# A decoder layer in fp32: attention summed by parts, and eight gate tiles moved ahead of it

## The reference

```python
z = jnp.einsum('bhqd,bhkd->bhqk', qb, kb).astype(jnp.float32) * scale
mask = kpos < qpos
log_beta = jax.nn.log_sigmoid(z)
log_1m_beta = jnp.where(mask, jax.nn.log_sigmoid(-z), 0.0)
log_a = log_beta + lax.cumsum(log_1m_beta, axis=3, reverse=True) - log_1m_beta
a = jnp.where(mask, jnp.exp(log_a), 0.0)
outs.append(jnp.einsum('bhqk,bhkd->bhqd', a.astype(vb.dtype), vb))
...
g = jax.nn.sigmoid(gate_logits.astype(jnp.float32)).astype(u.dtype)
g_pool, g_sb = jnp.split(g, 2, axis=-1)
return (g_pool * y_pool + g_sb * y_sb) @ w_out
```

## Time and profile before

| | us |
|---|---|
| median of 3 runs (lowest, highest) | 1923.49 (1922.86, 1924.46) |
| the profiled execution, its own time | 1924.59 |
| its span in the profile | 1922.6 |
| TensorE busy | 1908.7 |
| VectorE busy | 1399.9 |
| ScalarE busy | 789.2 |
| GpSimd busy | 152.4 |

### The profile page before, as it was taken

The page is one execution under the profiler, slowest core; times in us unless marked ns, Lnnn a source line. Parts: engine busy times, 40 slices in busy tenths (PEclk is TensorE's granted clock), DMA queues, the critical chain, the costliest instruction groups (busy, mean ns, idle before and its releaser), DMA issues.

```text
span 1922.6 us, 25206 instructions
## 1 busy us (share of the span) xinstructions
PE 1908.7 (99%) x9034; PEld 1596.7 (83%) x9034; DVE 1399.9 (73%) x1723; ACT 789.2 (41%) x1175; POOL 152.4 (8%) x221
## 2 busy tenths in 40 slices
PE   9999999999999999999999999999999999999998
PEld 9888888888888888888888888898888888888886
DVE  6977867774566776786878878889777777755655
ACT  7423232323434543345566652474323232334344
POOL 1000000000000300002443420010000000000002
PEclk9999999999999999999999999999999999999999
DMA  5456654558676534248546347643545444677665
GB/s 165 147 198 228 225 175 149 190 194 310 206 241 197 185 110 149 74 134 231 147 120 182 101 148 254 198 137 114 183 140 198 148 168 153 221 262 242 204 195 199
DMA packets 246724, 347.19 MB, mean 181 GB/s; under 512 B 16368, under 2 KB 150256, under 8 KB 243056
## 3 DMA queue, kind: packets, MB, share of 16 engines
q1 hardware_dynamic: 246640, 346.10, 55.0%
HBM read 232.79 MB, written 112.98 MB: 180 GB/s over the span
## 4 chain that ended last, share of the span: by engine, by line
PE 95%; DVE 3%; issue 1%; DMA 1%; ACT 0%; POOL 0%; SPq 0%; DVEq 0%; POOLq 0%; ACTq 0%
PE bank L1248 39%; PE bank L1357 10%; PE bank L1304 9%; PE bank L1305 9%; PE bank L1306 9%; PE bank L1498 4%; PE bank L1200 3%; PE bank L1406 2%; PE bank L1434 2%; PE bank L1464 2%; PE bank L1570 2%; PE bank L1175 1%; PE bank L1589 1%; PE bank L1588 1%; PE bank L1555 1%; PE bank L1553 1%
## 5 line engine op out<-in xcount | busy, mean ns | idle before, releaser
L2232 DVE TENSOR_TENSOR dn_lo<-dn_lo_raw,dn_hi 128x1024 fp32r<-128x1024 f32 x149 | 181.9, 1223 | 150.5 <-ACT dn_hi L1773 149.9
L1248 PE MATMUL bank<-lo_t,wa_hi 128*128 128x512 f32 x656 | 252.8, 389 | 0.0
L1248 PE MATMUL bank<-hi_t,wa_lo 128*128 128x512 f32 x656 | 252.8, 389 | 0.0
L1248 PE MATMUL bank<-hi_t,wa_hi 128*128 128x512 f32 x656 | 252.8, 389 | 0.0
L1773 ACT ACTIVATE dn_hi<-dn_lo_raw 128x1024 fp32r<-128x1024 f32 x149 | 157.9, 1061 | 218.3 <-DMA dn_lo_raw<-act_dram 218.3
L1304 PE MATMUL bank<-dn_hi 128*128 128x512 f32 x596 | 232.6, 390 | 0.0
L1306 PE MATMUL bank<-dn_lo,dn_hi 128*128 128x512 f32 x596 | 231.9, 389 | 0.0
L1305 PE MATMUL bank<-dn_hi,dn_lo 128*128 128x512 f32 x596 | 231.9, 389 | 0.0
L1248 PE MATMUL bank<-hi_b,wa_hi 128*128 128x512 f32 x492 | 190.7, 390 | 1.8 <-DVE up L2366 1.8
L1248 PE MATMUL bank<-lo_b,wa_hi 128*128 128x512 f32 x492 | 190.4, 389 | 0.0
L1248 PE MATMUL bank<-hi_b,wa_lo 128*128 128x512 f32 x492 | 190.4, 389 | 0.0
(11 more groups left out here) (276 smaller groups left out, 3722.7 us busy)
## 6 DMA issues: line engine op xcount, KB each, us to landing
wa_lo_raw<-in_ffn_w_gate_up_dram SPq DMA_DIRECT2D x87, 512.0 KB, 5.0
dn_lo_raw<-act_dram SPq DMA_DIRECT2D x149, 256.0 KB, 4.4
act_dram<-g SPq DMA_DIRECT2D x44, 512.0 KB, 4.3
wd_t<-in_ffn_w_down_dram SPq DMA_DIRECT2D x44, 512.0 KB, 6.6
act_dram<-s_of SPq DMA_DIRECT2D x88, 256.0 KB, 6.5
wd_dram<-wd_t SPq DMA_DIRECT2D x22, 1024.0 KB, 6.0
dn_lo_raw<-wd_dram SPq DMA_DIRECT2D x85, 256.0 KB, 3.3
dn_lo_raw<-in_ffn_w_down_dram SPq DMA_DIRECT2D x64, 256.0 KB, 3.0
```

Source lines behind the costliest of these rows:

```text
L1248: last = nc.tensor.matmul(acc, lhs, rhs, start=n == 0 and i != 2 and i < 5, stop=n == 11, skip_group_check=True)
L2232: return nc.vector.tensor_tensor(dst, raw, hi.bitcast(f32), ALU.subtract)
```

## The change

Three things are changed.

1. Summation by parts. In place of the weight of each key, its running sum from the right is made: one scan over `keep` and `a` (r = keep * r + a), written over `a`. The products then take differences of neighbouring values, v[s] - v[s-1], in place of the values. So `weigh_keys` loses its product, GpSimd masks `a` alone, the values are stored whole in DRAM behind a row of zeros (`v_dram`), and are loaded with and without a shift by one row (`load_v`), subtracted (`differences`) and split (`differences_hi`, `differences_lo`), for each of the four pairs of heads.
2. `EARLY = 8`: the eight tiles of the attention gate are made by four more units of seven products in `MIX_UNITS`, ahead of attention. In attention stand the eight tiles of the pooling gate, in four units of two tiles (`GATE_UNITS`), 16 banks. `SHARE` is changed, and still sums to 788 with the rest.
3. In the second feed-forward part, VectorE's second pair of units is written out as `second_pair`, with another order in its first unit.

```diff
-EARLY = 0
+EARLY = 8
 GATE_UNITS = tuple(((0, j), (0, j + 1)) for j in range(0, EARLY, 2)) + tuple(((0, j), (1, j)) for j in range(EARLY, KT))
...
+V_DIFF, V_HIGH, V_LOW = ({NT + 3 + d: 1, 3 * NT + 3 + d: 2, 5 * NT + 3 + d: 3} for d in (0, 1, 5))
...
-SHARE = {7: 8, 6: 16, 1: 16, 0: 11, 5: 4, 4: 12, 3: 13, 2: 12}
+SHARE = {7: 8, 6: 14, 1: 14, 0: 11, 5: 10, 4: 11, 3: 12, 2: 12}
...
-        v_dram = nc.dram_tensor("v_dram", (2, P, 2 * SEQ), f32, kind="Internal").ap()
+
+        v_dram = nc.dram_tensor("v_dram", (1 + SEQ, BR, P), f32, kind="Internal").ap()
...
+            def load_v(k):
+
+                if k >= 2:
+                    sp_.wait_ge(pv_ok, NT * (k - 1))
+                elif k == 0:
+                    for i in range(4):
+                        sp_.wait_ge(v_sp[i], 32)
+                    for i in range(3):
+                        sp_.wait_ge(ring_sp[i], 32 * ring_uses(i))
+                    sp_.wait_ge(ylo, 4)
+                    sp_.wait_ge(v_in[0], 16)
+                for a, row in ((0, 1), (1, 0)) if k >= 2 else ((1, 0),):
+                    for e in range(2):
+                        sp_.dma_start(v_raw[:, k % 2, :, e, a, :],
+                                      v_dram[row:row + SEQ, PAIR_ORDER[k], e * HD:(e + 1) * HD].rearrange("(t p) c -> p t c", p=P)
+                                      ).then_inc(v_in[k % 2], 16)
...
-                for pair in range(2):
-                    if s == NT * (2 + 2 * pair) + 4:
-                        load_v(pair)
+                for k in (1, 2, 3):
+                    if s == (2 * NT * (k - 1) + 4 if k > 1 else 2):
...
-                if x_["pair"] < 2 and pn % NT == 0:
-                    pe.wait_ge(v_in[slot], 16)
+                if pn % NT == 0:
+                    pe.wait_ge(v_split, 3 * (pn // NT) + 3)
...
-                nc.scalar.activation(v_w[:, :, t, :, 0, :], acc[:, 1], ACT.Copy)
-                if t > 4:
-                    act.wait_ge(v_sp[b], 16)
-                nc.scalar.activation(value_place(t)[:, :, :, 0, :], acc[:, 0], ACT.Copy).then_inc(ev_hi, 1)
+                nc.scalar.activation(v_raw[:, :, t, :, 0, :], acc[:, 1], ACT.Copy).then_inc(ev_hi, 1)
...
+            def differences_hi(k):
+
+                act.wait_ge(v_split, 3 * k + 1)
+                nc.scalar.activation(v_w[:, k % 2, :, :, 0, :], v_raw[:, k % 2, :, :, 1, :], ACT.Copy).then_inc(v_split, 1)
...
+                if s in V_HIGH:
+                    differences_hi(V_HIGH[s])
...
+                    second_pair(even, odd, units)
+                    with dve.Fori(2, KF - 2) as i:
                         pair_units(i, wd_use(1, i - 1))
...
+            def second_pair(even, odd, units):
+
+                c11(1, 2, 0)
+                weight_sums(1, 3, odd, units + 2)
+                c22_first(1, 2, 0)
+                weights_lo(1, 3, odd)
+                c22_second(1, 2, 0)
                 sums_of_pair(1, 0, lambda: dve.wait_ge(summed, 7 * strassen(1, 1) + 7))
+                sums_lo(1, 3, odd)
+                unit_end(1, 2, 1, 0, wd_use(1, 0))
+                up_unit(1, 3, 1, 1, more=(even, units + 3))
 
...
-                acc = bank[:, (t + 4) % 8, :].rearrange("p (m s e c) -> p m s e c", m=2, s=2, e=2)
-                nc.vector.tensor_tensor(v_w[:, :, t, :, 1, :], acc[:, 1], v_w[:, :, t, :, 0, :].bitcast(f32), ALU.subtract)
-                nc.vector.tensor_tensor(value_place(t)[:, :, :, 1, :], acc[:, 0], value_place(t)[:, :, :, 0, :].bitcast(f32),
-                                        ALU.subtract).then_inc(acc_free[t % 4], 1)
+                if t > 4:
+                    dve.wait_ge(v_sp[t % 4], 16)
+                nc.vector.tensor_copy(value_place(t), bank[:, (t + 4) % 8, :]).then_inc(acc_free[t % 4], 1)
...
+            def differences(k):
+
+                slot = k % 2
+                dve.wait_ge(v_in[slot], (32, 96)[k // 2] + (0 if slot else 16))
+                now, before = (v_raw[:, slot, :, :, a, :] for a in range(2))
+                nc.vector.tensor_tensor(before, now, before, ALU.subtract).then_inc(v_split, 1)
+
+            def differences_lo(k):
+
+                slot = k % 2
+                dve.wait_ge(v_split, 3 * k + 2)
+                nc.vector.tensor_tensor(v_w[:, slot, :, :, 1, :], v_raw[:, slot, :, :, 1, :],
+                                        v_w[:, slot, :, :, 0, :].bitcast(f32), ALU.subtract).then_inc(v_split, 1)
...
-                dve.wait_ge(masked, 2 * n + 2)
-                if n:
-                    dve.wait_ge(a_ok, n)
-                nc.vector.tensor_tensor_scan(tail_p[:, 0:w][:, ::-1], keep[:, n % 2, 0:w][:, ::-1],
-                                             zero_col[:, :].to_broadcast([P, w]), 1.0, ALU.mult, ALU.add).then_inc(scan_ok, 1)
-                dve.wait_ge(scan_ok, n + 1)
-                b = weights_of(n)[:, 0:w - 1]
-                nc.vector.tensor_tensor(b, b, tail_p[:, 1:w], ALU.mult).then_inc(a_ok, 1)
+                dve.wait_ge(masked, n + 1)
+                row = weights_of(n)[:, 0:w][:, ::-1]
+                nc.vector.tensor_tensor_scan(row, keep[:, n % 2, 0:w][:, ::-1], row, 0.0, ALU.mult, ALU.add).then_inc(a_ok, 1)
...
-                for dst, fill in ((keep[:, n % 2, w - P:w], 1.0), (weights_of(n)[:, w - P:w], 0.0)):
-                    nc.gpsimd.affine_select(out=dst, in_=dst, compare_op=ALU.is_gt, fill=fill, base=0,
-                                            pattern=[[-1, P]], channel_multiplier=1).then_inc(masked, 1)
+                last = weights_of(n)[:, w - P:w]
+                nc.gpsimd.affine_select(out=last, in_=last, compare_op=ALU.is_gt, fill=0.0, base=0,
+                                        pattern=[[-1, P]], channel_multiplier=1).then_inc(masked, 1)
```

More of the change, by code:

```diff
@@ L345, in macaron_layer @@
         sg2 = at("sg2", [P, 2, HALF], f32, base + 108 * K)
[L347 removed]
+        v_w, v_raw = both("v_w", [P, 2, NT, 2, 2, HD], X0)
         ring_raw = [at(f"ring_raw{i}", [P, SEQ], f32, X0 + 8192 * RING_AT[i]) for i in range(3)]
@@ L366, in macaron_layer @@
         k_lo2 = at("k_lo2", [P, 2, SEQ], f32r, o + 24576)
-        tail_p = at("tail_p", [P, SEQ], f32, o + 16384)
         gst = at("gst", [P, 2, HALF], f32, o + 20480)
@@ L521, in macaron_layer @@
         masked = sem("masked")
-        scan_ok = sem("scan_ok")
+        v_split = sem("v_split")
         a_ok = sem("a_ok")
@@ L978, in _ @@
                     pool_branch_unit(2)
+            load_v(0)
             spill_pool_branch(0)
@@ L1017, in load_head @@
                         sp_.dma_start(q_st[half, slot, c0:c1].bitcast(f32), qk_dram[part, pair, rows, c0:c1]).then_inc(quarter_in if hn == 0 and c0 == 0 else landed, 16)
-            def load_v(pair):
-                for i in range(4):
-                    sp_.wait_ge(v_sp[i], 32)
-                sp_.wait_ge(pv_ok, NT * (pair + 1))
-                sp_.dma_start(v_w[:, pair].rearrange("p t e a c -> p (t e a c)").bitcast(f32), v_dram[pair]).then_inc(v_in[pair], 16)
             load_head(0)
@@ L2133, in betas @@
                 if n >= 2:
-                    act.wait_ge(scan_ok, n - 1)
+                    act.wait_ge(a_ok, n - 1)
                 if n >= 3:
@@ L2967, in _ @@
                     pool_weight_sums(u + 2)
+                if u == 1:
+                    differences(0)
+                if u == 2:
+                    differences_lo(0)
             def weights_of(n):
@@ L3017, in _ @@
                     split_piece(j, piece)
+                if s in V_DIFF:
+                    differences(V_DIFF[s])
+                if s in V_LOW:
+                    differences_lo(V_LOW[s])
             def outputs_sum(i):
```

20 lines of the change are left out of this document (12 added, 8 removed).

## The result

The changed kernel takes 1943.93 us (1943.53 to 1946.27, 4 runs), the kernel before 1923.35 us (1922.86 to 1924.46) in the same comparison: ratio 1.0107, 95% interval [1.0095, 1.0119]. It is 1.1% slower. I had forecast 1934 us, 0.5% slower, with a range of 1912 to 1947.

The account below looks back on a forecast made before the run. TensorE was taken to bound the kernel, by instruction count times pace plus waits. Attention falls from 283.0 to 218.4 us, added units cost 75.9, so +11.3; with -0.9 elsewhere, +10.4, giving 1934 us, range 1912 to 1947.

Parts of the forecast that it names:

- the heads: Attention's seven head periods, turning of T4 to turning of T4: 25.2 us each, 176.4 us in all.
- the back: Attention from the last turning of T4 to the first branch product: 13.3 us, against 14.62 before.
- the front: Attention's start to the first turning of T4: 28.7 us, against 38.55 before.
- The trade on TensorE: 384 gate products leave attention, 336 come ahead of it: net 48 fewer, 10.8 us; the added units cost 75.9 us.
- The costs put at nothing: VectorE's and ScalarE's value differences, smaller value loads and three new queue waits, in attention: taken as zero.
- the case without cover: Value differences in attention if VectorE's idle time does not hide them: 8 x 1.23 = 10 us.
- the rival of a dearer scan: In-place scan pays for its second stream; two attention stretches grow, 2.2 us a head, +17.5, 1951 us; chance 0.13.
- All hidden: Rival: every attention chain stays covered by TensorE's work, so nothing new waits; 1911 us; chance 0.21.
- only leg 1: Rival: of four attention stretches only the first makes TensorE wait; 1923.5 us, no change; chance 0.20.
- the four don't overlap, so they add: Four stretches of each attention head where TensorE waits for chains: 1.1, 0.5, 0.4, 0.4, summed to 2.5 us a head.
- leg 1: In each attention head, from turning T4 to weighing (T4, T3): 5.1 us left against a chain of 6.2; wait 1.1.
- The second feed-forward part: Pair sums and weights_lo move behind c22_first, so TensorE's wait of 0.89 us goes: -0.9 us.

Follow-up runs that it names:

- Experiment 1: Parts alone: the changed kernel with all sixteen gate tiles left in attention (EARLY = 0) and the old SHARE; 1920.04 us, ratio 0.998 to the kernel before.
- experiment 9: The changed kernel with ScalarE's part of the value differences (differences_hi) one step later; 1938.80 us, ratio 1.0073 to the kernel before.
- experiments 3: The changed kernel with gate products put on one side of weighing and turning in four of a head's eight steps; 1945.03 us, ratio 1.0114 to the kernel before.
- experiment 4: The changed kernel with seven of every 24 gate products in attention left out; 1944.95 us, ratio 1.0107 to the kernel before.
- gates alone (2): The kernel before with only the gates moved (EARLY = 8, new SHARE), product of weights kept, no second pair; 1980.03 us, ratio 1.0291 to the kernel before.
- half scan, fewer gates (6): The changed kernel with running sums over the right half of keys only and seven of 24 attention gate products left out; 1926.11 us, ratio 1.0011.
- experiment 8: The changed kernel with the ten loads of outputs (O_STEP) issued two steps later; 1941.93 us, ratio 1.0096 to the kernel before.
- experiment 7: The changed kernel with four gate tiles moved ahead of attention instead of eight (EARLY = 4); 1917.78 us, ratio 0.9965 to the kernel before.

## Why the prediction came out as it did

The sign was right, and so was the reason at large: TensorE loses its cover. The size was half: 10.4 us on the profiled execution, where 19.0 were measured. Of the 8.7 us between, 4.7 lie in the heads, 3.4 in the back and 1.9 in the front, and the rest of the program gave back 1.5. The steps one by one.

**The trade on TensorE was right.** 48 instructions fewer, 76.1 us for the added units against 75.9.

**The costs put at nothing were nothing while TensorE covered them.** Experiment 1 holds them all (scan in place, differences, loads, SyncE's queue) and is faster than before. In the changed kernel one of them shows: ScalarE's copy of the differences, 1.06 us in three heads. One step later, in experiment 9, it costs these heads 2.6 us less together. For the case without cover I had priced VectorE's eight operations, but not ScalarE's four. The in-place scan is 2.29 us, so the rival of a dearer scan is out. "All hidden" is out by 20 us of waits, "only leg 1" by the same.

**The step that failed is "the four don't overlap, so they add".** I took four stretches out of a head, each with its own slack, and left the rest as free. The sum of 2.5 us a head (2.4 from the rounded terms) came near the measured 25.87 - 22.7 = 3.2, of which TensorE's rows show 2.3 as waits, and leg 1 fits (0.67 to 1.02 us shown, and a hand-over; 1.1 forecast). But experiments 3 and 4 show that the picture is wrong: moving 11 products a head into the legs gained nothing, taking 12 out cost nothing. What they show in its place is one floor a head, of the ring of hand-overs as a whole. It moved with VectorE's work:

| kernel | period, us | VectorE busy, us | the difference |
|---|---|---|---|
| gates alone (2) | 30.80 | 24.5 | 6.3 |
| changed kernel | 25.87 | 19.1 | 6.8 |
| fewer gates (4) | 25.87 | 19.1 | 6.8 |
| half scan, fewer gates (6) | 23.62 | 14.4 | 9.2 |

The floor rose by 4.93 us with 5.37 us more of VectorE's work (part of it may be the slower clock), and fell by 2.2 with 4.7 less. What limits the last row is open; ScalarE's 17.7 us and 5.9 of hand-overs would fit.

Two things these runs don't settle. The product and the half scan change VectorE's load and the length of each tile's chain together, so which of the two sets the floor is not separated; experiment 9, where three heads shortened with every engine's work as it was, says that load alone doesn't. And the difference of 6.3 to 6.8 us is measured in two kernels, with nothing to say what it is made of.

Here the leg picture happened to be 0.7 us a head short, 4.7 us in seven. The same picture was 19 us off in experiment 2, where the chains were longer. So the forecast of the heads was near for a reason that doesn't carry.

**Front and back were mis-sized by the clock and a queue.** Front: 28.7 forecast, 30.55 measured. The keys' second half came later (a wait of 2.56 us), and this was then paid again. The windows of the changed kernel from 948 us:

```profile
948.00:952.00 4.00, 1.75 (x7) 0.80 (x5) 0.74 (x2) 1.08 (x2) 0.29 (x1) 1.00 0.83 248
952.00:956.00 4.00, 2.99 (x9) 2.38 (x10) 1.10 (x1) 1.60 (x3) 0.00 (x0) 0.77 1.03 322
956.00:960.00 4.00, 4.00 (x18) 3.30 (x17) 2.18 (x3) 1.96 (x4) 0.29 (x1) 0.80 0.97 241
```

After two waits of 0.7 and 2.56 us the granted clock is 0.77 and 0.80 for 8 us. In experiment 8 the same front had waits of 1.28 and 0.31 us, stayed at 1.00 and took 27.39 us: 1.7 us less of waits and 1.5 us less of slow clock. In experiment 9 it took 29.7. The code of the three is the same up to there, so the front varies by 3 us with the waits for the first keys and the clock behind them, and 28.7 lies within that.

Back: 13.3 forecast, 16.7 measured. By experiment 7, where 13.62 us held hardly a wait for it, the chain was sized well for an undisturbed back. Of the 3.1 us between, 2.1 are the store behind the ten loads: the last copy of an output comes 6.6 us after the turning of T4 and not 4.55, and some 9.1 follow it. The other 1.0 is what the slow clock adds beyond that. The prediction named no cost for these loads, though their step is worked out from the number of gate banks and so moved by two.

**The second feed-forward part** gave 1.5 us where I had 0.9; another 0.9 is the landing of the last store (6.4 us from the last row of `h` to the end of the span, 7.3 before). The change has no part in that: it is 6.4 in experiment 2 too, with the old code there.

## What to carry to other kernels

Before work is taken from the engine that bounds a loop, find the loop's floor without it. Here that is about 25.9 us of 32.6 with parts alone, so 6.7 us a head could go, some 30 gate products, and the change took 45. What leaves above the floor can be gained; what leaves below it is lost, wherever it stands. The first four tiles gained 2 us, the next four lost 26. The trace with cover doesn't show the floor: with parts alone VectorE is busy for 20.1 us a head and idle for 12.5, and nothing in it tells how much of that idle time is hand-overs. A run with some of the work left out, as in experiment 4, does. And look at every place that is computed from the number that is changed: `O_STEP` and the step in which the first bank ends each made a wait of several us.
